# Two conditioned blocks on one core: from weights stationary to tokens stationary, 512 columns moving

## The reference

```python
mod = (silu(c) @ w_ada[l] + b_ada[l]).reshape(B, 9, D_MODEL)
h = rms_norm(x, gain) * (1 + scale) + shift
x = x + 0.5 * gate * ((silu(h @ w_gate) * (h @ w_up)) @ w_down)      # FFN, inner width 2816
# first mixer: chunked attention (8 heads), pooling, forgetting attention (8 heads),
#   three gated branches, then @ w_out
# second mixer: depthwise convolution branch, dilated-window attention (24 heads in 3 groups),
#   two gated branches, then @ w_o
```

## Time and profile before

| what | us |
|---|---|
| three timed runs | 3079.17, 3083.66, 3085.49 |
| median | 3083.66 |
| span of the profiled execution | 3078.6 |
| PE busy (of the span) | 2966.8 (96%) |
| DVE busy | 2104.4 (68%) |
| ACT busy | 1268.0 (41%) |
| DMA | 642.48 MB, mean 209 GB/s |

### The profile page before, as it was taken

The page is one execution under the profiler, slowest core; times in us unless marked ns, Lnnn a source line. Parts: engine busy times, 40 slices in busy tenths (PEclk is TensorE's granted clock), DMA queues, the critical chain, the costliest instruction groups (busy, mean ns, idle before and its releaser), DMA issues.

```text
span 3078.6 us, 59148 instructions
## 1 busy us (share of the span) xinstructions
PE 2966.8 (96%) x23231; PEld 2866.8 (93%) x23231; DVE 2104.4 (68%) x2869; ACT 1268.0 (41%) x1500; POOL 4.8 (0%) x28
## 2 busy tenths in 40 slices
PE   6999999999899999999999999999999999999998
PEld 5999988999899998899999999889989999998998
DVE  6767755876766775776776776567667677656766
ACT  2434335433334434543443443454334343345433
POOL 0000000000000000000000000000000000000000
PEclk9999989999899998999999999999999999999999
DMA  8776742576687662467677667536766766753674
GB/s 285 239 252 229 225 143 98 183 261 215 204 276 252 221 204 89 154 220 242 225 232 232 212 223 234 178 108 224 231 218 218 232 212 225 234 190 104 227 232 164
DMA packets 534450, 642.48 MB, mean 209 GB/s; under 512 B 12571, under 2 KB 500579, under 8 KB 534275
## 3 DMA queue, kind: packets, MB, share of 16 engines
q1 hardware_dynamic: 521151, 628.18, 62.3%
q10 hardware_dynamic: 13124, 11.93, 1.3%
HBM read 638.95 MB, written 8.97 MB: 210 GB/s over the span
## 4 chain that ended last, share of the span: by engine, by line
PE 89%; DVE 5%; issue 3%; ACT 2%; DMA 1%; DVEq 0%; SPq 0%; ACTq 0%
PE pair L1169 19%; PE pair L1170 18%; PE pair L1171 18%; PE acc L1169 8%; PE acc L1171 8%; PE acc L1170 8%; PE acc L1328 2%; PE small L1369 2%; PE stat L1248 2%; PE small L1241 2%; DVE temp L937 1%; DVE rstd L805 1%; ACT w_high L444 1%; DVE w_low L758 1%; PE small L1231 1%
## 5 line engine op out<-in xcount | busy, mean ns | idle before, releaser
L1169 PE MATMUL pair<-h_high,w_high 128*128 128x256 f32 x4480 | 1295.7, 289 | 17.1 <-DVE h_low L812 12.9
L758 DVE TENSOR_TENSOR w_low<-raw,w_high 128x2048 fp32r<-128x2048 f32 x433 | 990.2, 2290 | 467.5 <-ACT w_high L444 466.7
L1170 PE MATMUL pair<-h_low,w_high 128*128 128x256 f32 x4480 | 1280.1, 286 | 0.0
L1171 PE MATMUL pair<-h_high,w_low 128*128 128x256 f32 x4480 | 1279.8, 286 | 0.0
L444 ACT ACTIVATE w_high<-raw 128x2048 fp32r<-128x2048 f32 x434 | 826.5, 1906 | 293.6 <-PE acc L1171 256.1
L1169 PEld LDWEIGHTS pair<-h_high,w_high 128*128 128x128 f32 x4480 | 872.8, 195 | 27.9 <-issue 27.4
L1170 PEld LDWEIGHTS pair<-h_low,w_high 128*128 128x128 f32 x4480 | 873.3, 195 | 0.0
L1171 PEld LDWEIGHTS pair<-h_high,w_low 128*128 128x128 f32 x4480 | 872.2, 195 | 0.0
L1169 PE MATMUL acc<-y_high,w_high 128*128 128x256 f32 x1792 | 510.0, 285 | 4.0 <-DVE y_low L908 4.0
L775 DVE SCALAR_TENSOR_TENSOR ada_raw<-ada_raw,now 128x256 f32<-128x256 f32 x1008 | 488.8, 485 | 36.0
L1171 PE MATMUL acc<-y_high,w_low 128*128 128x256 f32 x1792 | 508.5, 284 | 0.0
(11 more groups left out here) (165 smaller groups left out, 2398.2 us busy)
## 6 DMA issues: line engine op xcount, KB each, us to landing
ada_raw<-in_w_ada_all SPq DMA_DIRECT2D x150, 1024.0 KB, 7.4
raw<-in_w_in SPq DMA_DIRECT2D x128, 1024.0 KB, 5.3
raw<-in_ffn_gate_all SPq DMA_DIRECT2D x89, 1024.0 KB, 5.4
raw<-in_ffn_up_all SPq DMA_DIRECT2D x89, 1024.0 KB, 5.4
raw<-in_ffn_down_all SPq DMA_DIRECT2D x88, 1024.0 KB, 5.3
raw<-in_w_branch SPq DMA_DIRECT2D x12, 1024.0 KB, 5.0
raw<-in_w_out SPq DMA_DIRECT2D x8, 1024.0 KB, 4.9
raw<-in_w_conv_out SPq DMA_DIRECT2D x8, 1024.0 KB, 5.0
```

Source lines behind the costliest of these rows:

```text
L758: nc.vector.tensor_tensor(w_low[:, slot, :], raw[:, slot, :], w_high[:, slot, :].bitcast(F32), ALU.subtract).then_inc(w_low_ready.sem, 1)
L1169: mm(dst, a_h, b_h, start=start, stop=False, skip_group_check=True)
L1170: mm(dst, a_h, b_l, start=False, stop=False, skip_group_check=True)
L1171: return mm(dst, a_l, b_h, start=False, stop=True, skip_group_check=True)
```

## The change

All products with weights change sides where they can. x, h and the mixers' intermediate results are kept token-major (128 tokens on the partitions, two token tiles `tt`). 128 x 128 pieces of h or y, taken by token tile, are stationary, and 512 columns of the weights move. So a gate or up chunk is now half the rows (four row tiles) of 512 columns, and two chunks make a block; the FFN has five blocks of 512 inner channels and one of 256 (`BLOCKS`). Channel-major results are still needed by the convolution and by q and k of the second mixer: those 24 chunks a stage keep the old form (`channel_unit`).

The norm is now per token: ACT squares with a sum along the free axis, the root is of one number a token. h is turned to channel-major by PE transposes, and so is the hidden product of each FFN block. `mean_square` and `clear_acc` are gone.

The modulation vectors are now spread over all partitions, 512 values at a time ("pairs", here called vectors 0 to 5 of a stage): a load of 2 MB into the one buffer `ada_raw`, eight DVE operations of 512 columns, and one PE product with a matrix of ones. Tables say behind which chunk of a stage each is summed (`SUM_AT`), multiplied (`ADA_AT`) and, six chunks behind that, loaded. `raw` has two slots instead of three, and `w_both` holds four split chunks instead of three.

At a stage's end the products of token tile 0 come first, then those of tile 1; update, norm and turning of tile 0 stand between. The loops are gone: every stage is written out.

```diff
-FFN_CHUNKS = 3 * TRIPS
-COLS = (2 * 2 * TRIPS + 26, 2 * 2 * TRIPS + 38)
+SLOTS = 4
+STAGES = [("f", ("a", "b")[layer // 2], "f")[sub] for layer in range(4) for sub in range(3)]
+UNITS = {"f": 33, "a": 36, "b": 48}
+BLOCKS = (512, 256, 512, 512, 512, 512)
...
+ADA_AT = {"f": {UP[1]: 0, UP[2] + 1: 1, UP[3] + 1: 2, DOWN[2] + 1: 3, UP[4] + 1: 4, UP[5] + 1: 5},
+          "a": {3: 0, 8: 1, 12: 2, 16: 3, 19: 4, 29: 5},
+          "b": {3: 0, 7: 1, 17: 2, 28: 3, 31: 4, 35: 5}}
+SUM_AT = {"f": {3: 0, 8: 1, 13: 2, 17: 3, 20: 4, 26: 5},
...
-        raw = sb("raw", [P, 3, 2048])
-        ada_raw = sb("ada_raw", [P, 2, 2048])
+        raw = sb("raw", [P, 2, 2048])
+        w_both = sb("w_both", [P, SLOTS, 2, 2048], F32R)
+        ada_raw = sb("ada_raw", [P, 8, 512])
...
-                sp.wait_ge(w_low_ready.sem, w_low_ready.at(at, n - 2, extra))
+                if n >= 2:
+                    sp.wait_ge(low_ready.sem, n - 1)
...
+            for s, kind in enumerate(STAGES):
+                places = {k + 6: p + 1 for k, p in ADA_AT[kind].items()}
+                for k in range(2, UNITS[kind] + 2):
+                    if k < UNITS[kind]:
+                        load(s, k)
+                    elif s < 11:
+                        load(s + 1, k - UNITS[kind])
+                    if k == 4:
+                        load_pair(s, 0)
+                    if k in places and places[k] < len(ada_pairs(s)):
+                        load_pair(s, places[k])
...
+            def high(s, k):
...
+                act.wait_ge(raw_landed[n % 2].sem, 16 * (n // 2 + 1))
+                if n >= SLOTS:
+                    act.wait_ge(used.sem, n - SLOTS + 1)
...
+            def begin(s):
+                if s:
+                    update(s - 1, 0, 0)
+                    update(s - 1, 0, 1)
+                norm(s, 0)
+                if s:
+                    update(s - 1, 1, 0)
+                if s < 12:
+                    low_of_h(s, 0, 0)
+                    low_of_h(s, 0, 1)
...
+            def block_unit(s, k, tt, dst, part=0, parts=2, fresh=False):
+                split = 8 // parts
+                wh, wl = weights(s, k, split)
+                for kk in range(split):
...
+                    last = triple(dst, h_high[:, tile, tokens(tt)], h_low[:, tile, tokens(tt)],
+                                  wh[:, kk, :], wl[:, kk, :], tile == 0)
...
+            def ada(s, k):
+                p = ADA_AT[STAGES[s]].get(k)
...
+                pe.wait_ge(ada_part.sem, ada_part.at(s, 8 * (p + 1)))
...
+                mm(ada_bank(s, p), ones, ada_raw[:, 0, :], start=True, stop=True, skip_group_check=True
+                   ).then_inc(ada_used.sem, 1)
```

More of the change, by code:

```diff
@@ L79 @@
[L79 to L101, removed]
@@ new lines, in ada_pairs @@
+        def ada_pairs(s):
+            layer = s // 3
+            own = [("gate", layer, (3 * (s % 3) + 2) * D + 512 * j) for j in range(2)]
+            if s == 11:
+                return own
+            after, sub = (s + 1) // 3, (s + 1) % 3
+            return (own + [("shift", after, 3 * sub * D + 512 * j) for j in range(2)]
+                    + [("scale", after, (3 * sub + 1) * D + 512 * j) for j in range(2)])
+        first_bias = [gate_all[0:1, :], temp[0:1, 0:1024]]
+        first_places = [flat(ada_raw[:, :, :]), proj_f[:, 0:4096], proj_f[:, 4096:8192], flat(ada_raw[:, :, :])]
@@ L727, in _ @@
+            for tt in range(TT):
+                norm(12, tt)
         @block.gpsimd
@@ L753, in _ @@
+            pool.memset(seed[:, :], 0.0).then_inc(zeros_ready.sem, 1)
         @block.vector
         def _(dve):
[L755 to L759 removed]
+            tensor = nc.vector.tensor_tensor
@@ new lines, in sum_pair, with scale_ready @@
+            def sum_pair(s, k):
+                p = SUM_AT[STAGES[s]].get(k)
+                if p is not None and p < len(ada_pairs(s)):
+                    for tile in range(8):
+                        sum_step(s, p, tile)
+            def scale_ready(s, k):
+                p = ADA_AT[STAGES[s]].get(k)
+                if p is None or p >= len(ada_pairs(s)) or ada_pairs(s)[p][0] != "scale":
+                    return
+                dve.wait_ge(ada_used.sem, ada_used.at(s, p + 1))
+                dve.wait_ge(gain_landed.sem, gain_landed.at(s, 16))
+                g = scale_all[:, 512 * (p % 2):512 * (p % 2) + 512]
+                fused(out=g, in0=ada_bank(s, p), scalar=1.0, in1=g, op0=ALU.add, op1=ALU.mult
+                      ).then_inc(mod_ready.sem, 1)
@@ L1235, in ada @@
-            def ada(at, u, slot, part_extra=None, extra=None):
-                pe.wait_ge(ada_part.sem, ada_part.at(at, DT * (u + 1), part_extra))
-                pe.wait_ge(ada_copied.sem, ada_copied.at(at, u, extra))
-                for i in range(2):
-                    last = mm(small[:, 2 * slot + i:2 * slot + i + 1], ada_raw[:, slot, P * i:P * i + P],
-                              ones[:, :], start=True, stop=True, skip_group_check=True)
-                last.then_inc(ada_used.sem, 1)
```

2509 lines of the change are left out of this document (1314 added, 1195 removed).

## The result

The changed kernel takes 3226.43 us (four runs, 3224.31 to 3231.55) where the kernel before takes 3083.94 beside it: a ratio of 1.0471 (95% interval 1.0456 to 1.0486), slower by 4.7%. I had forecast slower, 3127, with a range that ended at 3210: the direction was right, the size was not, and the time lies beyond the range. The profiled execution has a span of 3224.2, 145.6 more than before.

The account below looks back on a forecast made before the run. PE's own pace (busy 96%) was taken as the bound. The terms, 3078.6 + 7 x 15.0 - 6.5 - 24 - 6 - 11.5 - 14, gave 3122, with 5.1 for timed runs 3127 us; range 2950 to 3210.

Parts of the forecast that it names:

- start: Kernel start: fewer modulation vectors, half the sums on PE, no turning of x; first product near 51 us, not 74.9: -24.
- four mixers: Both mixer kinds: small savings less waits for sums and scale; -3 for each first, -4 for each second: -14.
- last FFN and end: Last FFN with only vectors 0 and 1, -6.5; end without mean square and turning back, tile 0 leaving early, -6.
- the loops' second trips: Unrolling drops all engines' waits at the loops' second trip, 5.75 us each, twice: -11.5.
- the spacing: PE's interval between 512-column fp32r products: taken as 0.216 us, between bounds of 0.213 and 0.227.
- rival C: Slower still: 0.227 per 512-column product adds 97 us on PE, or slot lateness sums over a stage: 3170 to 3230; chance 0.14.
- The FFN walk: One FFN stage followed in instruction order: 184.0 of PE work plus waits and slow clock, 220 us, 15.0 more than before.
- Chunk 5: FFN stage: rests and sum 0 on DVE delay the low part of tile 1's first hidden block; PE stalls 7 us.
- Behind chunk 18: FFN stage: PE waits for vector 3, whose load stands behind chunk 22's load; stall at least 10.5, taken as 14 us.
- The start: FFN stage start: PE idles 5.0 us through update and norm, plus 2.5 for chunk 3 and tile 1's h.
- The slow clock: FFN stage: after idle gaps PE runs at clock 0.5 for about 3 us, 1.6 lost; three gaps, 5 us.
- Rival A's turning point: Rival A (shorter waits, 3018 us, chance 0.26) wins once stalls behind chunk 18 and at chunk 5 together fall under some 14.

Follow-up runs that it names:

- run 2: Changed kernel with each 512-column product made as two of 256: 3292.72 us (1.0671 to the kernel before); 66 us more, of 119 put on PE.
- run 1: Separate small program, not the kernel: series of 64 PE products with operands ready; 512 columns of fp32r come every 0.227 us, of bf16 0.216.
- run 3: Changed kernel with its ten table stores issued from ACT's queue instead of SP's: 3227.76 us (1.0464 to the kernel before).
- run 8: Changed kernel with seven eighths of each modulation vector's load and sum left out: 2971.09 us (0.9641 to the kernel before).
- run 11: Changed kernel with modulation loads, sums and products placed anew and table stores spread over five FFN stages: 3034.8 us (0.9845 to the kernel before).
- run 12: Against run 11, eight of ten table stores moved into the first mixers' attention, vectors 4 and 5 used later: 2977.07 us (0.9653 to the kernel before).
- run 10: Changed kernel loading every modulation vector whole but making one of each sum's eight operations: 3036.49 us (0.9851 to the kernel before).
- run 5: Changed kernel with loads of vectors 1 to 5 issued five chunks behind the previous vector's use, not six: 3188.15 us (1.034 to the kernel before).

## Why the prediction was wrong

By its own terms, in us against the kernel before, each from first weight product to first weight product (the 11.5 of the loops taken out of the third and ninth stage):

| term | predicted | measured |
|---|---|---|
| start | -24 | -18.5 |
| five FFNs without table stores | +75 | +78.5 |
| first and fourth FFN | +30 | +64.4 |
| four mixers | -14 | +38.2 |
| last FFN and end | -12.5 | -5.4 |
| the loops' second trips (in the third and ninth stage) | -11.5 | -11.5, set by the earlier trace rows, not measured apart |
| sum | +43 | +146 |

**The largest step that failed is the spacing**, "I take 0.216"; the table stores, put at nothing, are the second, and the mixers' waits the third. 0.216 measured 0.227, the upper bound I had named, and rival C had it at 3170 to 3230; I gave it 0.14 and cut its end off. It weighs 8832 x 0.011 = 97 us on PE, which nearly equals the whole miss (99 us), but that is partly chance: by the 56% of run 2 it is about 54 at the end. That estimate and the 33 of the table stores leave 12 of the 99, the balance of errors both ways. In the table above the spacing stands in no row of its own: in the FFNs other errors offset it, in the mixers they add to it. The nearest row by length was bf16; the nearest by kind was the fp32r row, which carries the 0.013. Kind would have been the better choice, and my reason against it, that a load takes 0.12, doesn't hold: the earlier trace rows have transposes every 0.11, each with its load, and run 1 has 0.111. The Trainium skill ("TensorE: Matmul & The Clock Gate", Back-to-back issue gap) gives about 216 ns for an isolated and about 131 for a sustained product of 512 columns; this trace disagrees with both for fp32r (227 in a series), and run 1 has 216, not 131, in a bf16 series.

**Missed altogether: the table stores.** The kernel before has them in the same two stages at no cost (the earlier trace rows and the fourth stage above, 206.15), since PE was the bound. Now these stages take 238.3 and 237.5 for 221.4, 33 together. I had costed only what the change moves, and not what it leaves in place and uncovers. Run 3 shows that the queue they stand in is not the reason. Run 8 keeps 28 of the 33 with most of the modulation gone and has a weight load behind a store landing after 12.2 us: what they delay is the weights. Runs 11 and 12 show that they cost less in attention.

**The mixers** were off by 52. 120 of their 168 chunks take the new form (36 in each first, 24 in each second mixer), which puts 32 us on PE at 0.227. The rest, as I read it, is waits for sums that I had set equal to those gone, in stages where DVE has heads and merges to do besides; run 10 takes 23 and 27 us off the first mixers and 13 and 16 off the second by leaving the sums out.

**The FFN walk was right in its mechanism**, and near in size by two errors that offset each other. Chunk 5: 7 predicted, 5.9 to 6.5 measured. Behind chunk 18: 14 predicted, 11.2 to 12.7 measured in the five FFNs without stores, by the chain forecast: the sum of vector 2 ahead of chunk 18's rest, then load, split, vector, sum. The start was smaller, 3.9 of waits for 7.5, and there were hardly any for vectors 2, 4 and 5 (2.5 forecast). The slow clock was about as forecast: PE is busy 199.3 in the seventh stage (clock 0.95) and 193.9 in the same stage of run 12 (clock 1.00), 5.4 for 5. Against what was too long stand 31 x 24 x 0.011 = 8.2 of spacing. The sum 220 met 220.9 to 223.9.

**Start and end.** The first product comes at 56.38, not near 51. PE's last modulation work at the start ends at 45.1, where I had the last vector summed near 41, and it then waits 8.6 for the norm.

The forecast that PE would fall well under 90% busy was borderline (89%). Rival A's turning point (the two stalls together under 14 us) is what run 5 tests halfway: 11.3 in the seventh stage, and still 3188, since mixers and tables are not in it.

## What to carry to other kernels

When a tuned kernel's bound engine is made faster, the places in the other engines' programs that were free before are priced anew: list every transfer and block of work that shares a queue or engine with the supply, also those that the change doesn't touch. A load and the operation that uses it sit in two orders written out by hand; each has to stand behind the same piece of work, or the earlier one gains nothing. And take a bound's likeliest value from the row of the same kind of operation, not of the same length.

## What the hardware showed that I had not expected

At clock 1.0 an fp32r product has 0.013 us on top of its columns at 512, 384 and 256 columns, with the same stationary operand (loaded anew each time) or another, and in one bank or two in turn; bf16 has 0.003; at clock 0.5 fp32r has nothing on top (0.427 for 512 columns, run 1). Ten broadcasts of 768 KB cost 33 us in two stages through either queue (run 3), 28 of them with most of the modulation left out (run 8), 3 to 4 us each in an FFN of run 11, and 1 to 2 each in the attention of a mixer (run 12).
